# Token-mixer projections by a seven-product scheme, with norm, centring and variance products between the pairs

## The reference

```python
h = rms_norm(x, norm1_gain) * (1.0 + sc1) + sh1          # (2048, 1024); sc1, sh1 from c @ w_ada
p = h @ w_in                                             # eight projections of 1024 columns, and 256 low-rank ones
plain, rw = p[..., :N_PLAIN], p[..., N_PLAIN:]
rw = rw + (token_shift(rw) - rw) * token_mu
cb, cc, ch, ga, gb = split(plain)
y_conv = cb * causal_dwconv(cc * ch, conv_w)
r, k, v, wd, ad, gd = split(rw)
a = sigmoid(a0 + ad @ aaa_up);  g = sigmoid(gd) @ gate_up    # decay likewise from wd
kk = heads(k * k_k);  kk = kk / max(sqrt(sum(kk * kk)), 1e-12)
k = k * (1.0 + (a - 1.0) * k_a)
y = wkv7(r, decay, k, v, kk, a)                          # recurrence over the tokens, per head
mu = mean(y);  var = mean(square(y - mu))
yn = (y - mu) * rsqrt(var + LN_X_EPS) * ln_x_w + ln_x_b
y_rwkv = (yn + sum(r * k * r_k) * v) * g
merged = sigmoid(ga) * y_conv + sigmoid(gb) * y_rwkv;  mix = merged @ w_out
```

## Time and profile before

| | |
|---|---|
| three runs | 4534.02, 4536.60 and 4541.14 us; median 4536.6 |
| profiled execution | span 4533.3 us, first to last instruction; no other time of its own is listed |
| PE busy | 4221.6 us (93%), 33115 records |
| DVE, ACT, POOL busy | 1555.1, 1275.0, 301.5 us |
| DMA | 628.06 MB, mean 139 GB/s |
| stages | preamble to about 138 us, steps to about 2994 us, then output, router and experts |

### The profile page before, as it was taken

The page is one execution under the profiler, slowest core; times in us unless marked ns, Lnnn a source line. Parts: engine busy times, 40 slices in busy tenths (PEclk is TensorE's granted clock), DMA queues, the critical chain, the costliest instruction groups (busy, mean ns, idle before and its releaser), DMA issues.

```text
span 4533.3 us, 84111 instructions
## 1 busy us (share of the span) xinstructions
PE 4221.6 (93%) x33115; PEld 2214.5 (49%) x33115; DVE 1555.1 (34%) x3077; ACT 1275.0 (28%) x2803; POOL 301.5 (7%) x391
## 2 busy tenths in 40 slices
PE   7999999999999999999999999999959999999992
PEld 4455555555555555555555555555534444444440
DVE  3333433343344344433433343332441111111115
ACT  5233333333333333333333333333311111111113
POOL 0000100010000001000100000000000000000003
PEclk9999999999999999999999999989969999999996
DMA  9101000100100100100100100024359999999999
GB/s 331 46 6 41 19 11 28 32 9 21 37 13 9 49 8 14 49 9 13 47 11 9 51 9 11 6 94 148 111 222 411 411 411 411 411 411 411 411 411 378
DMA packets 250988, 628.06 MB, mean 139 GB/s; under 512 B 11410, under 2 KB 96628, under 8 KB 250612
## 3 DMA queue, kind: packets, MB, share of 16 engines
q1 hardware_dynamic: 231956, 555.46, 32.6%
q0 software_dynamic: 11520, 41.95, 2.4%
q10 hardware_dynamic: 7136, 25.23, 1.4%
HBM read 561.75 MB, written 60.84 MB: 137 GB/s over the span
## 4 chain that ended last, share of the span: by engine, by line
PE 89%; issue 4%; DVE 3%; DMA 2%; ACT 1%; SPq 1%; POOL 0%; DVEq 0%; ACTq 0%; POOLq 0%
PE bank L957 39%; PE bank L1313 10%; PE bank L1317 5%; PE bank L1343 5%; PE bank L1183 5%; PE bank L1347 2%; PE duo L1081 2%; PE duo L1079 2%; PE duo L1058 2%; PE duo L1052 1%; PE bank L1015 1%; PE duo L1294 1%; PE bank L999 1%; PE duo L894 1%; PE duo L1092 1%
## 5 line engine op out<-in xcount | busy, mean ns | idle before, releaser
L957 PE MATMUL bank<-hT,w 128*128 (+1 forms) x4096 | 1788.4, 593 | 0.0
L957 PEld LDWEIGHTS bank<-hT,w 128*128 128x128 f32 x4096 | 776.3, 190 | 990.4 <-issue 990.4
L1313 PE MATMUL bank<-W,xT 128*128 128x512 f32 x1024 | 446.9, 594 | 2.2 <-DVE xT L2283 1.5
L1379 ACT ACT_TABLE_LOAD x254 | 325.9, 1283 | 25.4 <-DVE ub L1961 14.3
L1313 PEld LDWEIGHTS bank<-W,xT 128*128 128x128 f32 x1024 | 192.8, 191 | 233.5 <-issue 233.5
L2289 DVE TENSOR_TENSOR gsig<-bank,gsig 128x512 f32<-128x512 f32 x48 | 33.2, 691 | 673.9 <-ACT gsig L1379 673.9
L1317 PE MATMUL bank<-W,xT 128*64 128x512 f32 x1024 | 228.7, 601 | 17.0 <-issue 17.0
L1183 PE MATMUL bank<-wo,mT 128*128 128x512 f32 x512 | 233.2, 602 | 0.0
L1343 PE MATMUL bank<-W,aT 128*128 128x512 f32 x512 | 225.1, 593 | 0.0
L733 POOL TENSOR_TENSOR Tm<-Tm,idents 128x512 f32<-128x512 f32 x32 | 40.5, 1266 | 2749.0 <-DVE Tm L1998 2749.0
L1379 ACT ACTIVATE gsig<-bank 128x512 f32<-128x512 f32 x48 | 28.7, 598 | 659.1 <-PE bank L1313 424.0
(11 more groups left out here) (374 smaller groups left out, 5531.9 us busy)
## 6 DMA issues: line engine op xcount, KB each, us to landing
W<-in_w_expert_in_dram SPq DMA_DIRECT2D x128, 2048.0 KB, 25.5
W<-in_w_expert_out_dram SPq DMA_DIRECT2D x64, 2048.0 KB, 25.3
w<-in_w_in_dram SPq DMA_DIRECT2D x64, 512.0 KB, 4.0
adaw<-in_w_ada_dram SPq DMA_DIRECT2D x12, 2048.0 KB, 12.8
y_s<-ysb ACTq DMA_DIRECT2D x48, 512.0 KB, 6.7
xt<-in_x_dram SPq DMA_DIRECT2D x16, 512.0 KB, 11.8
WAc<-rank_s SPq DMA_DIRECT2D x32, 256.0 KB, 3.2
GDc<-rank_s SPq DMA_DIRECT2D x32, 256.0 KB, 3.2
```

Source lines behind the costliest of these rows:

```text
L957: ins = mm(PJ[j % 2][:, :], w[:, j, k, :], hT[:, k, ds(group(i) * G, G)], start=k == 0, stop=k == KT - 1)
L1313: ins = mm(GU[half][:, :], xT[:, slot, kk_, :], ring_rows(parts[0])[:, k, cols], start=kk_ == 0, stop=kk_ == KT - 1)
L1379: return nc.scalar.activation(o, i, f, **kw)
```

## The change

**Seven products.** The eight projections form four pairs: (k, r), (v, ch), (cc, cb), (ga, gb). For a pair X, Y with weights split in halves of the 1024 input channels, and h split by the same halves and by halves of the 512 tokens, the 2 x 2 block product is made by seven products of 4 matmuls, each 128 x 256, after Winograd's form of Strassen's scheme. Four of the seven weight blocks are sums (S1 to S4), and four of the seven blocks of h (T1 to T4).
- Weight sums: POOL, `mix_weights`, four operations of 128 x 512 for each pair, once a turn, ahead of POOL's `seeds`.
- h: no longer kept in SBUF. In the preamble each group goes to one buffer `hg`; DVE makes the four sums (`mix_h`); SP writes the seven 512 KB blocks to DRAM (`save_h`), and `evac_x` of the next group waits for these. In the steps SP loads the seven blocks of the next group into `hs`, each as soon as the same product of the last pair has ended (`load_h`).
- Banks: pairs 0 and 2 use SA, SD, SC, pairs 1 and 3 use SB and PJ (`TRIO`); `place` gives a product's half bank. Products 4 to 6 add to the places of products 1 to 3, which have to be read first: product 4 waits for the first sum on DVE, product 5 for the third. Product 3 of pair 0 lies in SC and waits for `a_ready`.
- Sums: ACT copies product 1 (`half`), DVE makes the five sums (`begin_sums`, `second_of_y`, `second_of_x`, `first_of_y`), ACT copies or passes on the first half of X. Shift mixes read SBUF, since k, r and v now stand whole in `T3`.

**Order on PE.** norm and centred stand between pairs 1 and 2, variance between pairs 2 and 3, bonus and gup behind pair 3. **Order on DVE.** post stands behind the second and third sum of pair 2, ahead of `ub` and the conv steps.

```diff
-        hT = sb(main, "hT", [P, KT, T])
-        w = sb(main, "w", [P, 8, KT, P])
+        hs = sb(main, "hs", [P, NPROD, KH, GH])
+        w = sb(main, "w", [P, 4, NPROD, KH, P])
...
+        TRIO = [(SA, SD, SC), (SB, PJ[0], PJ[1])]
+        PLACE = ((0, 1), (0, 0), (1, 0), (2, 0), (0, 0), (1, 0), (2, 0))
...
+            def save_h(g):
+                sp.wait_ge(S["T_act"], 4 * g + 4)
+                sp.wait_ge(S["T_dve"], 4 * g + 4)
+                for slot, kh, th in ((U_B11, 0, 0), (U_B21, 1, 0), (U_B22, 1, 1)):
+                    sp.dma_start(h_s[g, slot].rearrange("p (k t) -> p k t", k=KH), h_quarter(kh, th))\
+                        .then_inc(S["h_saved"], 16)
+                sp.wait_ge(S["h_mix"], 4 * g + 4)
+                for j, slot in enumerate((U_T2, U_T1, U_T3, U_T4)):
+                    sp.dma_start(h_s[g, slot].rearrange("p (k t) -> p k t", k=KH), h_mixed(g)[:, j])\
+                        .then_inc(S["h_saved"], 16)
...
                 if not final:
+                    for n in range(NPROD):
+                        sp.wait_ge(S["proj_done"], prod_count(i, 3, n))
+                        load_h(nxt, n)
...
-                for k in range(KT):
-                    ins = mm(PJ[j % 2][:, :], w[:, j, k, :], hT[:, k, ds(group(i) * G, G)],
-                             start=k == 0, stop=k == KT - 1)
+            def proj(i, pr, n):
+                if n == 0:
+                    pe.wait_ge(S["w_step"], tile_no(i) * 16 + pr * 4 + 4)
...
+                if pr == 0:
+                    pe.wait_ge(h_in_sem[n], i * 16 + 16)
+                    if n == 3:
+                        pe.wait_ge(S["a_ready"], i + 1)
+                if n == 4:
+                    pe.wait_ge(S["summed"], sum_count(i, pr, 0))
+                if n == 5:
+                    pe.wait_ge(S["summed"], sum_count(i, pr, 2))
+                for k in range(KH):
+                    ins = mm(place(pr, n), w[:, pr, n, k, :], hs[:, n, k, :], start=n < 4 and k == 0,
+                             stop=k == KH - 1, skip_group_check=True)
                 ins.then_inc(S["proj_done"], 1)
...
             def head(i):
+                q = prior2(i)
                 zdec(i)
                 zaaa(i)
-                proj(i, 0)
-                proj(i, 1)
-                proj(i, 2)
+                pair(i, 0)
+                pair(i, 1)
                 norm(i)
-                proj(i, 3)
-                proj(i, 4)
+                if q is not None:
+                    centred(q)
 
             def tail(i, p):
                 q = prior2(i)
-                if q is not None:
-                    pe.wait_ge(S["P_step"], i * 2 + 2)
-                    centred(q)
-                proj(i, 5)
+                pair(i, 2)
                 if q is not None:
                     variance(q)
-                proj(i, 6)
+                pair(i, 3)
+                bonus(i)
                 gup(i)
-                proj(i, 7)
-                bonus(i)
                 inverse_and_recurrence(i, p)
...
             def evac_x(g):
+                if g:
+                    act.wait_ge(S["rank_done"], 2 * g)
+                    act.wait_ge(S["h_mix"], 4 * g)
+                    act.wait_ge(S["h_saved"], 16 * NPROD * g)
...
+            def begin_sums(i, pr):
+                dve.wait_ge(S["half_copied"], i * 4 + pr + 1)
+                V.tensor_tensor(su[:, 1], su[:, 0], place(pr, 0), ALU.add).then_inc(S["summed"], 1)
+
+            def second_of_y(i, pr, out):
+                dve.wait_ge(S["proj_done"], prod_count(i, pr, 3))
+                dve.wait_ge(S["summed"], sum_count(i, pr, 0))
+                V.tensor_tensor(su[:, 2], su[:, 1], place(pr, 3), ALU.add).then_inc(S["summed"], 1)
+                dve.wait_ge(S["summed"], sum_count(i, pr, 1))
+                V.tensor_tensor(out, su[:, 2], place(pr, 2), ALU.add).then_inc(S["summed"], 1)
```

More of the change, by code:

```diff
@@ L45 @@
         ("ga", 3 * D), ("gb", 4 * D)]
+PAIR_COLS = [(COLS[2 * n][1], COLS[2 * n + 1][1]) for n in range(4)]
+NPROD = 7
+KH = KT // 2
+GH = G // 2
+(U_T2, U_B11, U_T1, U_T3, U_B21, U_B22, U_T4) = range(NPROD)
+(W_S2, W_A11, W_S1, W_S3, W_A12, W_S4, W_A22) = range(NPROD)
+NSUM = 5
 (Q_MUR, Q_MUK, Q_MUV, Q_KK, Q_KA, Q_A0, Q_W0, Q_RK, Q_LNW, Q_LNB, Q_CW0, Q_CW1, Q_CW2, Q_N1, Q_OMR, Q_OMK,
@@ L201, in build @@
         p4 = ExitStack()
+        su = sb(p4, "su", [P, 3, GH])
+        cbb = sb(p4, "cbb", [P, G])
+        spare = sb(p4, "spare", [P, 1792])
         par = sb(p4, "par", [P, NQ])
@@ L544, in load_step @@
                 if turn:
-                    for j in range(6):
-                        sp.wait_ge(S["proj_done"], i * 8 + j + 1)
-                        load_col(j, ct + 1)
+                    for pr in range(3):
+                        sp.wait_ge(S["proj_done"], prod_count(i, pr, NPROD - 1))
+                        load_pair(pr, ct + 1)
                 if prior2(i) is not None:
@@ L552, in load_step @@
                 if not final:
+                    for n in range(NPROD):
+                        sp.wait_ge(S["proj_done"], prod_count(i, 3, n))
+                        load_h(nxt, n)
+                if turn:
+                    load_pair(3, ct + 1)
+                if not final:
                     sp.wait_ge(S["gup_done"], i + 1)
@@ L746, in seeds @@
                 hat(i, p, Kb, 5)
-            seeds(0, 0)
-            seeds(1, 1)
-            with pool.Fori(1, STEPS // 2) as h:
-                seeds(h * 2, 0)
-                seeds(h * 2 + 1, 1)
+            with pool.Fori(0, KT - 1) as ct:
+                for g in range(NG):
+                    if g == NG - 1:
+                        for pr in range(3):
+                            mix_weights(ct + 1, pr)
+                    seeds(ct * NG + g, g % 2)
+                mix_weights(ct + 1, 3)
+            for g in range(NG):
+                seeds((KT - 1) * NG + g, g % 2)
             pool.wait_ge(S["merged_out"], 16 * STEPS)
@@ L959, in proj, with pair @@
                 ins.then_inc(S["proj_done"], 1)
+            def pair(i, pr, ns=range(NPROD)):
+                for n in ns:
+                    proj(i, pr, n)
             def seq_ahead(q, c, p, xb=XB):
@@ L1491, in step, with half, first_half, scaled @@
                 act.wait_ge(S["carry_saved"], i + 1)
-                def scaled(m, q_mu):
-                    act.wait_ge(S["proj_done"], i * 8 + m + 1)
-                    fn(T3[:, m, 1:G + 1], PJ[m % 2][:, :], ACT.Copy, scale=par[:, q_mu:q_mu + 1])\
-                        .then_inc(S["shift_scaled"], 1)
+                def half(pr):
+                    act.wait_ge(S["proj_done"], prod_count(i, pr, 1))
+                    if pr:
+                        act.wait_ge(S["summed"], sum_count(i, pr - 1, 0))
+                    elif not first(i):
+                        act.wait_ge(S["summed"], sum_count(i - 1, 3, 0))
+                    fn(su[:, 0], place(pr, 1), ACT.Copy).then_inc(S["half_copied"], 1)
+                def first_half(pr, m):
+                    act.wait_ge(S["proj_done"], prod_count(i, pr, 4))
+                    fn(T3[:, m, 1:GH + 1], place(pr, 1), ACT.Copy).then_inc(S["first_out"], 1)
+                def scaled(m, t, q_mu):
+                    fn(t[:, :], T3[:, m, 0:G], ACT.Copy, scale=par[:, q_mu:q_mu + 1]).then_inc(S["shift_scaled"], 1)
                 act.wait_ge(S["zdec_done"], i + 1)
@@ L1503, in step @@
                 fn(at[:, :], SC[:, :], ACT.Sigmoid, bias=par[:, Q_A0:Q_A0 + 1]).then_inc(S["a_ready"], 1)
-                scaled(0, Q_MUK)
+                half(0)
+                first_half(0, 0)
+                act.wait_ge(S["first_out"], i * 3 + 1)
+                act.wait_ge(S["summed"], sum_count(i, 0, 3))
+                if not first(i):
+                    act.wait_ge(S["kk_ready"], i)
+                scaled(0, kt, Q_MUK)
+                act.wait_ge(S["summed"], sum_count(i, 0, 4))
+                if not first(i):
+                    act.wait_ge(S["operands"], i * 5 - 4)
+                scaled(1, rt, Q_MUR)
                 act.wait_ge(S["shifted"], i * 3 + 1)
```

226 lines of the change are left out of this document (158 added, 68 removed).

## The result

The changed kernel takes 4627.47 us (median of four runs, 4618.29 to 4634.43), the kernel before 4538.87 beside it: ratio 1.0192, 95% interval 1.0175 to 1.021, so about 89 us slower. The forecast was 4546 with a range of 4500 to 4595. The side was right, the size was not, and the measured time lies above the range. The side is no merit of the forecast either: it gave a loss of 9 us, which it called hardly measurable, and nearly all of the other 80 us come from terms that it put at nothing.

What follows compares the result with a forecast made beforehand. PE, 93% busy, was taken as the bound: 4533.3 - 210.6 + 116.7 + 2.8 + 31.5 - 10.5 + 54 + 25 = 4542.2, with 3.3 us outside the span 4546 us; range 4500 to 4595.

Steps and rivals of the forecast that it cites:

- Fewer columns: Projections on PE: 224 records of 216.0 ns a step instead of 128 of 429.4, -210.6 us; weight load stays hidden.
- New waits in the pairs: PE waits for DVE ahead of fifth and sixth products: 0.55, 2.87 and 0.47 us, +116.7 in 30 steps, +2.8 in first two.
- The wait for `at`: Step's start: fourth product of pair 0 waits for `at` 2.25 us in 14 even steps, +31.5 us.
- Preamble: Ahead of the first step: copies of h out and back move first zdec from 137.6 to 192 us, +54.
- Copies of h in the loop: Seven 512 KB loads a step cost nothing, since DMA is 1% busy and PE needs them some 30 us later.
- Clock: PE's clock falls after the 2.87 us wait in half of the steps, 15 x 1.7 = +25 us.
- The step that failed: POOL's 16 weight sums, 1.27 us each, once in four steps, ahead of its inverse work: cost nothing.
- A second term put at nothing: The inverse: some 29 us of small products a step that the change leaves alone, no cost given.
- the uniform 1 us a step for a slower DVE: Rival: each DVE operation 10% slower makes PE wait longer, 4578 us; kept as upper part of the main case.
- The clock's fall in nearly every step: Rival: PE's clock falls in nearly every step, also at the 2.25 us wait, 4597 us; chance 0.13.
- The two faster ones: Rivals: clock holds through the waits, 4521 us, chance 0.20; preamble hides its copies, 4517 us, chance 0.15.
- the exposed weight load: Rival: half the weight load shows at each shorter projection matmul, +358 us, 4904 us; chance 0.04.

Runs made afterwards that it cites:

- copies_part: Changed kernel with the preamble's copies of h to DRAM cut to a sixteenth of their bytes for groups 1 to 3; 4608.9 us, ratio 1.0151.
- combined_h_part: combined with each of the seven loads of h in a step cut to a quarter of its bytes; 4406.1 us, ratio 0.9701.
- store_last: combined with SP's store of mg put behind the seven loads of h instead of ahead of them; 4414.8 us, ratio 0.9741.
- small_sums: Changed kernel with POOL's weight sums in the steps' turns cut to one column each, order, waits and transfers kept; 4570.3 us, ratio 1.0072.
- pool_later: Changed kernel with POOL's full weight sums moved: pair 1's into DVE's idle time, those of pairs 2 and 3 behind the seeds; 4571.2 us, 1.0073.
- post_later: Changed kernel with DVE's order altered: u and conv steps ahead of post, pair 3's first sum inside post; 4534.4 us, ratio 0.9989.
- combined: Changed kernel with the edits of pool_later and post_later, zaaa in another bank, and pair 0's first copy and sum earlier; 4475.4 us, ratio 0.9849.

## Why the prediction was wrong, step by step

- **Fewer columns**: right. Inside a product at full clock the records start 215.8 ns apart, 216.0 was taken; the small excess belongs to each record. The weight load stays hidden, as costed, though with less room than walked: its record takes some 190 ns at full clock, in both kernels, and not half of the 206.
- **New waits in the pairs**: right in place for all steps, and close in size for the 23 of 30 without a turn: 0.26, 2.76 and at most 0.27 us against 0.55, 2.87 and 0.47. In the first two steps it is 0.92 each against 1.4.
- **The wait for `at`**: 25.2 us in 14 steps against 31.5, some 1.8 us each.
- **Preamble**: 58.3 us against 54, and copies_part shows the copies in its chain.
- **Copies of h in the loop, costed at nothing**: right for the changed kernel's pairs, but not free. Nothing in the forecast saw that transfers can delay instructions; combined_h_part and store_last put 52 to 69 us on it once they bunch.
- **Clock**: the place was right, the share roughly so. Behind the fifth product's wait a stretch at 1.2 GHz followed in 23 of 30 steps, not in 15: in 16 of the 23 with 2.76 us, and in all seven turns with 4.3 to 5.4. The share is no constant: with the same 2.76 us in all 30 steps it was 19 in small_sums and 13 in pool_later, so half was a fair guess for that pause, and lucky, since no row had one like it. Each costs less than the 1.7 us taken: an odd step without it takes 55.3 us from its first projection to its last, with it 56.4. Here are windows behind the wait in two steps (us, busy of each engine, PEclk, DMA share, GB/s); the clock stays full in the first and falls in the second:

```profile
1325.00:1330.80 5.80, 5.50 (x24) 4.56 (x25) 2.50 (x5) 0.80 (x2) 0.00 (x0) 1.00 1.00 340
1413.50:1420.30 6.80, 6.80 (x25) 5.35 (x25) 2.35 (x6) 1.00 (x3) 0.00 (x0) 0.83 0.98 350
```

- **The step that failed** is "The weight sums are 16 operations of POOL, 1.27 us each, once in four steps, some 8 us ahead of POOL's own work in the inverse: nothing." They were priced as time on POOL, which is idle, and as a wait of PE for the weights, which is hidden. Their price is what they do to DVE. Ahead of the inverse a turn takes 8.9 us more than another odd step, 62 us in seven. Of this the two waits are 3.35 and 2.4 us (7 x 5.75 = 40 us). The clock is also at half for 6.8 us more, which costs up to half of that time (7 x 3.4 = 24). Without the sums these 8.9 us are gone (small_sums: 58.5 against 58.8 us).
- **A second term put at nothing** is the turn's inverse, among the "small products that the change leaves alone". It takes 30.9 us and took 28.2 before, 7 x 2.7 = 19 us, and small_sums leaves it at 30.6. PE's pauses for instructions are longer there, 18.7 us in the seven turns against 4.6 before, beside queues filled by the weight loads that follow those of h.
- The rows chosen for the forecast don't show what POOL does to DVE, but the trace of before has one place. In the inverse, DVE and POOL each mask parts of LTb at the same time, both reading only SBUF, and DVE's operation, some 0.42 us long at best, takes 0.86 or more in 32 of its 64 cases (min, median and max in ns):

```profile
L2023 DVE TENSOR_TENSOR Qm<-LTb,m0Ts x64: 418/700/904, 202.2 to 2965.5; 64x256 f32<-64x256 f32 x64
```

- That spread, or the rule of the skill named above, would have asked for a walk of DVE's queue with POOL's sums in it.
- **The rivals**: the uniform 1 us a step for a slower DVE had the right engine, and spread over 32 steps what strikes seven. The clock's fall in nearly every step was half true: it came behind most waits of 2.76 us, but not behind those of 1.8. The two faster ones and the exposed weight load were false.

## What to carry to other kernels

Work given to an idle engine isn't free because that engine is idle. Ask what it shares with the engine that PE waits for, and put it where that engine rests or reads PSUM. When products are made to wait for an elementwise engine, walk that engine's whole queue, and start its longest chain early: one product moved inside a pair was worth 176 us here. In a queue of transfers, a store that waits ahead of prefetches turns them into a bunch, and a bunch can hold up PE's instructions. And when a step is priced as a mean, look for the few steps in which something else happens: here seven of 32 held nearly the whole miss.

## What the runs showed of the hardware

- DVE and POOL take turns when both read two operands from SBUF. DVE's 128x512 operation goes from 0.69 to between 1.4 and 1.75 us, POOL's from 1.27 to between 1.3 and 1.7. The 128x256 sum with a PSUM operand keeps 0.41. DVE's 128x512 operation with one SBUF tensor (L2152) went from 0.48 to 1.16.
- PE's instruction supply competes with bulk transfers. Its pause some 5 us into the inverse grew to as much as 4.8 us in post_later, where in the step shown the queues were full for 5.5 us, and stayed at 2.3 or less with a quarter of h's bytes. In each such pause PE went on 1.2 to 1.6 us after the end of a 16 KB packet of q8. The profile calls the pause issue. The Trainium skill, "Runtime: NRT & Kernel Launch", section "Instruction fetch mechanics", says that refills come as DMA and are mostly hidden; here they were not, behind such a bunch.
- The granted clock: pauses of 1.8 us between dense products were followed by half clock in two of 14 steps of post_later. The pause of 2.76 us was followed by it in 16 of 23 steps of the changed kernel and in 13 of 30 of pool_later. With neither, the 32 stretches ahead of the inverses in combined hold 10 us at half clock in all, against 125 in the changed kernel.
